# Normalising x on VectorE and turning it by the identity, and one FFN product moved ahead in a hybrid encoder layer

## What is computed

```
h   = RMSNorm(x) * g_pre_mix
z   = h @ w_in                      # 1024 -> 1440 mixer columns + 2048 gate columns
A   = multi-head latent attention,  B = sliding-window attention
m   = sum_b sigmoid(gate_b) * (branch_b @ w_branch[b])
x   = x + RMSNorm(m @ w_out) * g_post_mix
h2  = RMSNorm(x) * g_pre_ffn
gu  = h2 @ w_gate_up                # 1024 -> 2 x 2816
f   = (silu(gu[:, :2816]) * gu[:, 2816:]) @ w_down
out = x + RMSNorm(f) * g_post_ffn
```

## Time and profile before

| | |
|---|---|
| median of 3 runs | 913.73 us (912.53 to 913.86) |
| the profiled execution | 912.8 us, of which the core's span is 911.0 us |
| PE busy | 885.9 us, 97% of the span |
| DVE, ACT, POOL busy | 486.9, 389.1, 75.6 us |
| granted PE clock, mean | 0.997 of full |

### The profile page before, as it was taken

How to read it: one execution, slowest core, us unless ns; L and a number is a source line. 1 busy time by engine, 2 the same in 40 slices (tenths; PEclk the granted TensorE clock), 3 DMA queues, 4 the chain that set the end, 5 groups by cost and what they waited for, 6 DMA issues and landing times.

```text
span 911.0 us, 13815 instructions
## 1 busy us (share of the span) xinstructions
PE 885.9 (97%) x5521; PEld 805.4 (88%) x5521; DVE 486.9 (53%) x750; ACT 389.1 (43%) x771; POOL 75.6 (8%) x73
## 2 busy tenths in 40 slices
PE   7999999999999988999997999999999999999997
PEld 6888999999976867998787999999999998888885
DVE  6423532433354455564678877777777774343124
ACT  6211422435453655442665545444554543332112
POOL 0300198140030000000000000000000000000000
PEclk9999999999999999999999999999999999999999
DMA  7623246153330001655513233222333325222202
GB/s 270 180 69 87 67 123 188 44 169 90 100 70 1 2 1 32 206 179 188 182 71 92 70 93 93 79 78 77 94 93 93 93 72 239 84 70 93 70 24 115
DMA packets 101455, 91.97 MB, mean 101 GB/s; under 512 B 8480, under 2 KB 85296, under 8 KB 101248
## 3 DMA queue, kind: packets, MB, share of 16 engines
q1 hardware_dynamic: 95216, 86.45, 30.7%
q10 hardware_dynamic: 5280, 2.72, 1.1%
q0 software_dynamic: 896, 1.92, 0.7%
HBM read 79.60 MB, written 12.40 MB: 101 GB/s over the span
## 4 chain that ended last, share of the span: by engine, by line
PE 92%; ACT 3%; DVE 2%; DMA 1%; issue 1%; SPq 0%; ACTq 0%; DVEq 0%
PE ps L1153 27%; PE ps L1154 26%; PE ps L1155 26%; PE ps L1336 2%; PE ps L1204 1%; PE ps L1385 1%; PE ps L1347 1%; PE ps L1432 1%; PE ps L1306 1%; PE ps L1379 1%; PE ps L1310 1%; DVE nm_c L1718 1%; ACT probs L877 1%; PE ps L1407 1%; PE ps L1417 1%
## 5 line engine op out<-in xcount | busy, mean ns | idle before, releaser
L1644 DVE TENSOR_TENSOR wlo<-raw,whi 128x1024 fp32r<-128x1024 f32 x59 | 78.5, 1333 | 205.2 <-ACT whi L803 197.4
L803 ACT ACTIVATE whi<-raw 128x1024 fp32r<-128x1024 f32 x59 | 62.1, 1056 | 180.9 <-PE ps L1155 169.6
L1153 PE MATMUL ps<-h_hi,wlo 128*128 128x320 f32 x288 | 90.9, 316 | 0.8 <-DVE h_lo L1878 0.8
L1155 PE MATMUL ps<-h_hi,whi 128*128 128x320 f32 x288 | 88.9, 309 | 0.0
L1154 PE MATMUL ps<-h_lo,whi 128*128 128x320 f32 x288 | 88.9, 309 | 0.0
L1153 PE MATMUL ps<-sc_hi,t_lo 128*128 128x320 f32 x252 | 78.0, 309 | 3.9 <-ACT u L1068 2.9
L1154 PE MATMUL ps<-sc_lo,t_hi 128*128 128x320 f32 x252 | 77.8, 309 | 0.0
L1155 PE MATMUL ps<-sc_hi,t_hi 128*128 128x320 f32 x252 | 77.8, 309 | 0.0
L1058 ACT ACTIVATE t_hi<-wd 128x512 fp32r<-128x512 f32 x84 | 52.8, 629 | 58.6 <-DVE wd L1919 52.8
L1153 PE MATMUL ps<-whi,gu_lo 128*128 128x512 f32 x190 | 74.0, 390 | 0.4 <-DVE gu_lo L1991 0.4
L1155 PE MATMUL ps<-whi,gu_hi 128*128 128x512 f32 x190 | 73.9, 389 | 0.0
(11 more groups left out here) (305 smaller groups left out, 2145.0 us busy)
## 6 DMA issues: line engine op xcount, KB each, us to landing
raw<-in_w_gate_up SPq DMA_DIRECT2D x44, 512.0 KB, 3.8
raw<-in_w_down SPq DMA_DIRECT2D x22, 512.0 KB, 3.6
raw<-in_w_in SPq DMA_DIRECT2D x16, 512.0 KB, 4.2
raw<-in_w_in SPq DMA_DIRECT2D x12, 480.0 KB, 4.0
gates_scratch<-gate_s SPq DMA_DIRECT2D x16, 320.0 KB, 2.4
gate_r<-gates_scratch SPq DMA_DIRECT2D x8, 640.0 KB, 4.1
raw<-in_w_branch SPq DMA_DIRECT2D x8, 512.0 KB, 4.9
raw<-in_w_out SPq DMA_DIRECT2D x8, 512.0 KB, 5.5
```

The lines of the kernel that those rows point to most:

```text
L803: act.activation(whi[:, r % 2, :] if to is None else to, raw[:, r, :], ACT.Copy).then_inc(w_hi, 1)
L1153: pe.matmul(out, left[1], right[0], start=first, stop=False, skip_group_check=not own_group)
L1155: return pe.matmul(out, left[0], right[0], start=False, stop=last, skip_group_check=not own_group)
L1644: dve.tensor_tensor(lo[:, place, :], raw[:, r, :], hi[:, place, :].bitcast(F32), ALU.subtract).then_inc(w_lo, 1)
```

## The change

In the first stage the buffer `xg` and the diagonal are gone. DVE normalises x in place with one instruction (x by the reciprocal root by the gain), and PE turns `x_t` by the plain identity with transposes. The identity is turned 44 times at the start in place of 24. The turn of tile t+1 now stands in the middle of the products of tile t for every t, and the products wait for the first half tile alone (`h_lo_rdy` at 2t+1). On ACT the statistics of tile t+1 and the split of a weight slot stand between the copies of the two half tiles of tile t; on DVE the scaling of tile t+1 and the weight split stand between the two subtractions.

In the FFN GEMM m1 of pair 1 runs ahead of pair 0's second half (n = 1). Its weight split moves ahead of tile 4's copies on ACT and on DVE. Its PSUM result is read early into a buffer of its own (`u1_1`), behind a one-element Silu that computes nothing that is used. The splits, sums and differences of pair 1 are in another order: the differences m6, m7 and m4 are made one by one between the sums, m4's last, after `sum_lo(2)` and the split of m7's operand.

```
@@ -321,8 +321,6 @@
...
     x_t = area("x_t", [P, TILES, D], 10240)
-    xg = area("xg", [P, TILES, D], 20480)
-    diag_r = area("diag_r", [P, 2, P], 32800)
     junk_h = area("junk_h", [P, D], 27680)
...
@@ -406,6 +404,7 @@
...
     u1 = area("u1", [P, HALF], 14336)
+    u1_1 = area("u1_1", [P, HALF], 32768)
     u2 = [area("u2_0", [P, HALF], 14656), area("u2_1", [P, HALF], 16256)]
...
@@ -443,7 +442,7 @@
...
         eps_rdy, pad_rdy, const_rdy, sink_rdy = sem("eps_rdy"), sem("pad_rdy"), sem("const_rdy"), sem("sink_rdy")
-        h_ssq, h_sd, h_rs, h_xg, h_diag, h_tr, h_hi_rdy, h_lo_rdy = (sem(n) for n in ("h_ssq", "h_sd", "h_rs", "h_xg", "h_diag", "h_tr", "h_hi_rdy", "h_lo_rdy"))
+        h_ssq, h_sd, h_rs, h_norm, h_tr, h_hi_rdy, h_lo_rdy = (sem(n) for n in ("h_ssq", "h_sd", "h_rs", "h_norm", "h_tr", "h_hi_rdy", "h_lo_rdy"))
         table_rdy = sem("table_rdy")
...
@@ -825,18 +824,17 @@
...
             for t in range(TILES):
-                if t and t + 1 < TILES:
-                    h_stat(t + 1)
-                if t in (2, 3):
-                    split_hi(t, 16, in_hi[:, t - 2, :])
-                for n in (2 * t, 2 * t + 1):
-                    half = n % 2
+                for half in range(2):
+                    n = 2 * t + half
                     act.wait_ge(h_tr, n + 1)
...
                                    ps[:, 5 + n % 3, :].rearrange("p (k n) -> p k n", k=4), ACT.Copy).then_inc(h_hi_rdy, 1)
-                if t == 0:
-                    h_stat(1)
-                    split_hi(1, 16)
+                    if half == 0 and t + 1 < TILES:
+                        h_stat(t + 1)
+                    if half == 0 and t == 0:
+                        split_hi(1, 16)
+                    if half == 0 and t in (2, 3):
+                        split_hi(t, 16, in_hi[:, t - 2, :])
             act.dma_start(wuq_raw[:], w_uq[0].rearrange("(k p) n -> p k n", p=P)).then_inc(wuq_in, 16)
...
@@ -1044,8 +1042,6 @@
...
                                bias=eps_c[:, 0:1]).then_inc(h2_sd, 1)
-            h2_hi_copies(TILES - 1)
-
             def op_split_hi(m):
...
@@ -1065,7 +1061,7 @@
...
                         act.wait_ge(c11_rdy, p - 1)
-                    act.activation(u1[:], ps[:, bank, 0:HALF], ACT.Copy).then_inc(u1_rdy, 1)
+                    act.activation((u1 if p > 1 else u1_1)[:], ps[:, bank, 0:HALF], ACT.Copy).then_inc(u1_rdy, 1)
                 elif kind == "m6":
...
@@ -1084,17 +1080,20 @@
...
 
-            for m in range(3):
-                op_split_hi(m)
+            op_split_hi(0)
+            op_split_hi(1)
+            h2_hi_copies(TILES - 1)
+            op_split_hi(2)
+            act.activation(ssq_h[:, 7:8], eps_c[:, 0:1], ACT.Silu)
+            read_product(0)
             act.wait_ge(w_used, WO0 + 8)
-            sum_hi(0)
-            sum_hi(1)
+            for i in range(3):
+                sum_hi(i)
             act.wait_ge(sc_sum, 4)
             op_split_hi(3)
-            sum_hi(2)
+            op_split_hi(4)
             act.wait_ge(w_used, GU0 + 2)
             act.activation(silu_0[:].rearrange("p (n c) -> p n c", n=2), ps[:, 0:2, 0:HALF], ACT.Silu).then_inc(silu_0_rdy, 1)
-            op_split_hi(4)
             op_split_hi(5)
...
@@ -1103,7 +1102,8 @@
...
             for n in range(NP):
-                read_product(n)
+                if n:
+                    read_product(n)
                 if n + LEAD + 1 < NP - 1:
...
@@ -1194,30 +1194,26 @@
...
             def h_turn(t):
-                pe.wait_ge(h_xg, t + 1)
-                pe.wait_ge(h_diag, t + 1)
+                pe.wait_ge(h_norm, t + 1)
                 for n in (2 * t, 2 * t + 1):
...
                         c = (4 * (n % 2) + k) * P
-                        ins = pe.matmul(ps[:, 5 + n % 3, k * P:(k + 1) * P], xg[:, t, c:c + P], diag_r[:, t % 2, :],
-                                        start=True, stop=True)
+                        ins = pe.transpose(ps[:, 5 + n % 3, k * P:(k + 1) * P], x_t[:, t, c:c + P], ident[:])
                     ins.then_inc(h_tr, 1)
...
             pe.wait_ge(const_rdy, 1)
-            for n in range(24):
+            for n in range(44):
                 pe.transpose(ps[:, 7, 0:P], ident[:], ident[:])
...
             for t in range(TILES):
-                if t and t + 1 < TILES:
-                    h_turn(t + 1)
-                pe.wait_ge(h_lo_rdy, 2 * t + 2)
+                pe.wait_ge(h_lo_rdy, 2 * t + 1)
                 rows = slice(t * P, (t + 1) * P)
...
                     j, kk = divmod(k, 2)
-                    if t == 0 and k == 2:
-                        h_turn(1)
+                    if k == 2 and t + 1 < TILES:
+                        h_turn(t + 1)
                     if t == 0:
...
@@ -1225,6 +1221,7 @@
...
                         ins.then_inc(w_used, 1)
+            pe.wait_ge(h_lo_rdy, 2 * TILES)
 
...
@@ -1555,11 +1552,6 @@
...
             wide_half(1, h2_hi, h2_lo, 2, 0, KD // 2, KD)
-            pe.wait_ge(h2_lo_rdy, 2 * TILES)
-            pe.wait_ge(h2_raw, 2 * TILES)
-            pe.wait_ge(bank_empty, 25)
-            wide_half(0, h2_hi, h2_lo, 1, 1, 0, KD).then_inc(w_used, 1)
-            wide_half(1, h2_hi, h2_lo, 3, 1, 0, KD).then_inc(w_used, 1)
 
...
@@ -1598,7 +1590,13 @@
...
 
-            for n in range(NP):
+            pe.wait_ge(bank_empty, 25)
+            product(0)
+            pe.wait_ge(h2_lo_rdy, 2 * TILES)
+            pe.wait_ge(h2_raw, 2 * TILES)
+            wide_half(0, h2_hi, h2_lo, 1, 1, 0, KD).then_inc(w_used, 1)
+            wide_half(1, h2_hi, h2_lo, 3, 1, 0, KD).then_inc(w_used, 1)
+            for n in range(1, NP):
                 product(n)
...
@@ -1650,39 +1648,29 @@
...
 
-            def h_gain(t):
-                dve.wait_ge(x_in[t], 16)
-                dve.tensor_tensor(xg[:, t, :], x_t[:, t, :], gpre_b[:], ALU.mult).then_inc(h_xg, 1)
-
             def h_scale(t):
...
                 dve.wait_ge(h_rs, t + 1)
-                if t >= 2:
-                    dve.wait_ge(h_tr, 2 * t - 2)
-                dve.tensor_scalar(diag_r[:, t % 2, :], ident[:], r_h[:, t:t + 1], None, ALU.mult).then_inc(h_diag, 1)
-
-            dve.wait_ge(const_rdy, 1)
+                dve.scalar_tensor_tensor(out=x_t[:, t, :], in0=x_t[:, t, :], scalar=r_h[:, t:t + 1], in1=gpre_b[:],
+                                         op0=ALU.mult, op1=ALU.mult).then_inc(h_norm, 1)
+
             dve.wait_ge(gpre_in, 16)
-            h_gain(0)
             h_scale(0)
...
             for t in range(TILES):
-                if t and t + 1 < TILES:
-                    h_gain(t + 1)
-                    h_scale(t + 1)
-                if t in (2, 3):
-                    split_lo(t + 1, t, in_hi, in_lo, t - 2)
-                for n in (2 * t, 2 * t + 1):
-                    half = n % 2
+                for half in range(2):
+                    n = 2 * t + half
                     to = slice(4 * half, 4 * half + 4), slice(t * P, (t + 1) * P)
...
                                       h_hi[:, to[0], to[1]].bitcast(F32), ALU.subtract).then_inc(h_lo_rdy, 1)
-                if t == 0:
-                    h_gain(1)
-                    h_scale(1)
-                    split_lo(2, 1)
+                    if half == 0 and t + 1 < TILES:
+                        h_scale(t + 1)
+                    if half == 0 and t == 0:
+                        split_lo(2, 1)
+                    if half == 0 and t in (2, 3):
+                        split_lo(t + 1, t, in_hi, in_lo, t - 2)
             split_lo(5, 0)
...
@@ -1897,8 +1885,6 @@
...
                                          op0=ALU.mult, op1=ALU.mult).then_inc(h2_norm, 1)
-            h2_lo_parts(TILES - 1)
-
             def op_split_lo(m):
...
@@ -1941,25 +1927,25 @@
...
             op_split_lo(1)
-            for kind in DIFFERENCES:
-                difference(kind, 1)
-            op_split_lo(2)
-            dve.wait_ge(h2_raw, 2 * TILES)
+            difference("m5", 1)
+            h2_lo_parts(TILES - 1)
             dve.wait_ge(w_used, WO0 + 8)
             dve.tensor_tensor(sums(0), rows_at(1, 0), rows_at(1, 1), ALU.add).then_inc(sc_sum, 1)
+            op_split_lo(2)
+            difference("m6", 1)
             dve.wait_ge(sc_sum, 1)
             dve.tensor_tensor(sums(1), sums(0), rows_at(0, 0), ALU.subtract).then_inc(sc_sum, 1)
+            sum_lo(0)
             dve.tensor_tensor(sums(2), rows_at(0, 0), rows_at(1, 0), ALU.subtract).then_inc(sc_sum, 1)
...
             dve.tensor_tensor(sums(3), rows_at(0, 1), sums(1), ALU.subtract).then_inc(sc_sum, 1)
-            sum_lo(0)
+            sum_lo(1)
             op_split_lo(3)
-            sum_lo(1)
+            difference("m7", 1)
             dve.wait_ge(silu_0_rdy, 1)
...
             op_split_lo(4)
-            sum_lo(2)
             dve.wait_ge(sc_sum, 4)
...
@@ -1970,7 +1956,7 @@
...
                         dve.wait_ge(u_prod, 1)
```

(14 more changed lines are left out.)

## The result

| | before | changed |
|---|---|---|
| median of the runs | 913.8 us (912.53 to 914.1, 4) | 906.66 us (906.46 to 906.83, 4) |
| ratio | | 0.9925, 95% interval 0.9911 to 0.9939 |
| the profiled execution | 912.8 us, span 911.0 | 906.51 us, span 904.7 |
| PE busy | 885.9 us | 884.0 us |

The change is 0.75% faster. The profiled executions differ by 6.3 us. Here is the start of the changed kernel's timeline (start, duration, engine, line, operation, idle before; records from 14 us on are left out but for the turns and the stage's end), to be held against the earlier trace rows.

A forecast was written before the change was run, and what follows sets the result against it. The prediction took PE, busy for 97% of the span, as the bound. Gains of 3.3 us in the first stage and 3.1 in the FFN entry gave 913.7 - 6.4 = 907.3 us, range 905.3 to 910.2.

The forecast's parts named there:

- the sum: Whole kernel: 912.8 - 3.3 - 3.1 = 906.4 us for an execution like the profiled one.
- The start: First stage: products of tile 0 start at 10.77 us, not 13.15, 2.4 us gained; DVE's weight split ends last.
- The tiles: First stage: a loop of 4.30 us per tile replaces 4.4, PE waits some 0.7 us per tile; 0.9 us gained.
- The rival that I gave 0.32: First stage: the clock falls once, near 11.2 us or earlier, costing 1.0 to 1.3 us; 908.5 us, chance 0.32.
- The late rise: First stage: all 44 turns run slow, tile 0's turn starts 3.5 us late, no gain there; 910.6 us, chance 0.07.
- The FFN entry: FFN entry: m5 of pair 2 starts earlier, gain 3.1 us; of 5.4 us of waits some 2.2 come back.
- both new waits: FFN entry: PE waits 1.8 us before m7 for u2, then 0.4 us before m4 for u3.
- DVE decides: FFN entry: DVE's list from 484.2 us to the end of m4's difference takes 15.2 us, thus 499.4.
- no new wait: Rival, FFN entry: ACT reaches u2 in time, 1.8 us more gain; 905.5 us, chance 0.08.
- The median: Whole kernel: the profiled execution stays 0.9 us under the median of the runs, so 913.7 - 6.4 = 907.3 us.

The follow-up runs named there:

- e6: The changed kernel with ACT reading u2 and u3 ahead of splits and DVE adding to u3 one place earlier; 904.98 us, ratio 0.9910 to the kernel before.
- e7: The changed kernel with the turn of tile t+1 back ahead of the products of tile t, for t of 1 and more; 907.83 us.
- e11: The changed kernel with its turns as plain float32 products by the identity, two passes where a transpose has one; 908.65 us.
- e10: The changed kernel with the products of tile t waiting for both half tiles again; 921.24 us.
- the control: The changed kernel itself run once more, nothing altered, for its own spread; 906.75 us (905.63 to 908.23).
- the first stage alone: The kernel before with only the first-stage part of the change, FFN entry as before; 910.81 us, ratio 0.9973.
- e3: The changed kernel with ACT reading u2 of pair 1 ahead of the splits of m4's and m3's operands; 907.99 us.
- e5: The changed kernel with 24 turns of the identity at the start in place of 44; 907.56 us.

## Why the prediction was right, and where it was off

**Size and sign.** 907.3 was forecast, 906.66 came. Against the profile the sum was 906.4, and the profiled execution has 906.51. That this agrees to 0.1 us is luck in part: the first stage gave 2.8 and not 3.3, the FFN entry 3.2 for 3.1, and 0.3 us came in places that the sum doesn't name (0.1 between in_hi and the last turn of h2, 0.2 behind m5 of pair 2).

**The start.** In the profiled execution every link came within 0.1 us: normalised x to PE at 8.07 (8.08), first copy 8.76 (8.84), DVE's split at 8.84, first product 10.72 (10.77). What ends last is the weight split on DVE, as said. In other executions the turn of tile 0 comes later; more of that below.

**The tiles.** The loop is 4.22 us, where I had 4.30: ACT's copy begins a little sooner behind the turn. The waits on `x_t` are 0.2 to 0.6 us, not 0.7, and in the profiled execution only two of the four are left, as the low clock fills the others. With the clock whole from the start, as in the profile of e6, in_hi is at 29.97, 0.4 before my 30.4. The direction of the point stands: by e7 PE's products lie outside the loop, by e11 the first half of the turn lies in it, and by e10 a wait for DVE's second subtraction would set its pace.

**The clock.** The rival that I gave 0.32 came true in the profiled execution: it fell at 11.3 us and cost 30.93 - 29.97 = 0.96 us, my price being 0.95. The two errors, 0.4 too slow and 1.0 too fast, partly cancel, so the sum looks better than its terms.

The late rise, which I gave 0.07, is the common case. Of the ten profiles with 44 turns at the start, seven have the turn of tile 0 at 8.49 to 9.20 instead of 8.04 to 8.07. It costs what it delays: in the five of them that have the change's first stage, with fill turns or without, in_hi comes 21.9 us behind that turn, as in the profile of e6 (8.04 to 29.97). For the control that is 1.0 us, not the 3.3 that I gave it. The whole delay does go through, as I said, by ACT's copy and its statistics, though the first product moves by only 0.3 (11.06), since DVE's split covers the rest there. What was wrong is the size of the delay: I let all 44 turns run slow, and they sped up on the way. So of the profiles of the change's first stage with 44 turns and no fill, the one of e6 alone has the course that the sum assumes, a punctual turn and a whole clock. The fall and the late rise each put in_hi at 30.9 to 31.1, which is why the forecast holds about as well either way.

**The FFN entry.** Gain 3.2 forecast as 3.1, with both new waits at the places and nearly the sizes forecast (1.7 and 0.4 for 1.8 and 0.4). "DVE decides" was right only together with the place of ACT's reads. DVE's chain ended when I said (the difference for m4 at 496.5, 15.2 us behind 481.3), but that it was late mattered only because ACT had put the read of `u2` behind it. e6 shows the difference: same chain, no wait in pair 1. My rival "no new wait" priced that at 1.8 us, and e6 gave 1.8, though through 2.55 us gained and 0.7 lost again at m7 of pair 2, which I hadn't seen.

**The median.** I carried the profiled execution's 0.9 us below the median over to the new kernel. It didn't carry: the new median lies 0.15 above its profiled execution. With 0.1 us the other way in the sum, that is the 0.6 us by which the forecast is high. How far one execution lies from a median of three or four is mostly chance, so that term of the sum had no mechanism behind it.

## What to carry to other kernels

A wait that vanishes is replaced by the next one in line. Write out the in-order list of each helper engine behind it: what PE needs next must not be queued behind something that waits for a third engine. Reads of a product that frees its bank or feeds the next product belong ahead of splits for products further on; moving three such reads gave 1.8 us with no instruction added, and the next wait stood in the same queue one pair on. And where the helpers set the pace, cut tiles so that PE can start on the first part while they normalise the next.

## What the runs showed of the hardware

The spread of the kernel before between executions, 911.1 to 916.3 us, goes with the mean granted clock: 0.999 at 911.1 to 911.6, 0.996 or 0.997 at 912.0 to 913.3, 0.994 or 0.995 at 913.6 to 914.0, 0.992 or 0.993 at 915.0 and above (48 executions).

The same wait of PE can cost the full clock in one execution and not in another. The 2.9 us before m6 of pair 1 did in the profile of the first stage alone and not in that of the kernel before. The 1.6 us before the first product did in the changed kernel's profile (at 11.3 us) and not in that of e6. The clock also fell near 8 us in the kernel before, at 502 in e3, and near 347 us, in the attention part, in the profiles of e5, e6 and e7, where PE has several short waits in a row; here is e6:

```profile
346.00:349.00 3.00, 2.87 (x12) 0.51 0.01 3
```

A fall costs 1.0 to 1.5 us where a profile with it can be held against one without it: 0.96 at 11.3 us, 1.25 behind m6, 1.5 behind m4 in e3, and 1.3 at 347, where e6 takes 448.06 us from in_hi to the last turn of h2 and the control 446.79. So a part of what removing a wait gains can be in the wait, and a part in a fall that no longer happens. A single profile shows the one and may not show the other.

How fast PE is at the very start differs too. The 44 turns of the identity took 6.42 us in the changed kernel's profile and 7.63 in the control's, with PE at work on nothing else, and all that hangs on the first real turn moves with them.
